# Second attention of a two-block transformer kernel: a convolution moved into the first step, an inverse root merged, three steps shifted

## What is computed

```
h = concat([meta(16), pad, x]); h += concat([mla, diff, swa](rms_norm(h) @ w_in)) @ w_out
h += (silu(hn @ w_gate) * (hn @ w_up)) @ w_down;  x = rms_norm(h, final_norm)[meta:]
h = rmsnorm(x);  q, k, v = split(silu(causal_depthwise_conv(h @ w_qkv)))      # second block
o_dn = gated_deltanet(q, k, v, z, b, a)                                      # 8 heads of 128
o_ns = gates * (compressed, selected, window attention of 16 heads of 64)
x += (sigmoid(g1) * (o_dn @ w_dn) + sigmoid(g2) * (o_ns @ w_ns)) @ w_out
x += square(relu(rmsnorm(x) @ w_up)) @ w_down
```

## Time and profile before

| | us |
|---|---|
| median of 3 runs (lowest to highest) | 957.08 (955.95 to 958.02) |
| the profiled execution, its own time | 955.19 |
| its span, first to last instruction | 953.4 |
| PE busy | 922.3 (97%) |
| DVE busy | 636.9 (67%) |
| ACT busy | 466.9 (49%) |
| POOL busy | 156.2 (16%) |
| mean granted clock of TensorE | 0.991 |

### The profile page before, as it was taken

How to read it: one execution, slowest core, us unless ns; L and a number is a source line. 1 busy time by engine, 2 the same in 40 slices (tenths; PEclk the granted TensorE clock), 3 DMA queues, 4 the chain that set the end, 5 groups by cost and what they waited for, 6 DMA issues and landing times. The chain is left out here.

```text
span 953.4 us, 17694 instructions
## 1 busy us (share of the span) xinstructions
PE 922.3 (97%) x6958; PEld 828.8 (87%) x6958; DVE 636.9 (67%) x1338; ACT 466.9 (49%) x925; POOL 156.2 (16%) x111
## 2 busy tenths in 40 slices
PE   9999899999999999997799999999999999999998
PEld 8897688999999989886688888998888899999996
DVE  4657766666556687798997977545966665455543
ACT  6554655545344562753334674354453464454441
POOL 1100000000000015006565315000000022233221
PEclk9999999999999999999799999999999999999999
DMA  6830334556556445646232101022546546555651
GB/s 242 260 128 1 116 128 122 182 183 223 160 191 216 144 140 180 223 157 216 74 127 87 48 14 67 3 69 90 177 175 202 183 147 221 178 177 177 195 182 44
DMA packets 38578, 139.31 MB, mean 146 GB/s; under 512 B 4325, under 2 KB 4581, under 8 KB 38496
## 3 DMA queue, kind: packets, MB, share of 16 engines
q1 hardware_dynamic: 37152, 134.10, 42.9%
q10 hardware_dynamic: 816, 2.25, 0.7%
q0 software_dynamic: 528, 1.84, 0.7%
HBM read 137.09 MB, written 1.08 MB: 145 GB/s over the span
## 5 line engine op out<-in xcount | busy, mean ns | idle before, releaser
L1835 DVE TENSOR_TENSOR parts<-raw,parts 128x1024 fp32r<-128x1024 f32 (+2 forms) x225 | 286.6, 1310 | 131.7 <-ACT parts L1322 127.0
L1322 ACT ACTIVATE parts<-raw 128x1024 fp32r<-128x1024 f32 (+2 forms) x225 | 228.1, 1050 | 115.8 <-PE psum L532 96.3
L530 PE MATMUL psum<-hT,parts 128*128 128x256 f32 (+1 forms) x928 | 264.6, 285 | 14.4 <-DVE scr L2236 13.2
L531 PE MATMUL psum<-hT,parts 128*128 128x256 f32 (+1 forms) x928 | 263.4, 284 | 0.0
L532 PE MATMUL psum<-hT,parts 128*128 128x256 f32 (+1 forms) x928 | 261.6, 282 | 0.0
L530 PEld LDWEIGHTS psum<-hT,parts 128*128 128x128 f32 x928 | 175.5, 189 | 17.9 <-DVE scr L2236 13.4
L532 PEld LDWEIGHTS psum<-hT,parts 128*128 128x128 f32 x928 | 176.9, 191 | 0.0
L531 PEld LDWEIGHTS psum<-hT,parts 128*128 128x128 f32 x928 | 175.9, 190 | 0.6
L530 PE MATMUL psum<-parts,arena_r 128*128 128x512 f32 x344 | 135.1, 393 | 0.9 <-DVE arena_r L1850 0.7
L532 PE MATMUL psum<-parts,arena_r 128*128 128x512 f32 x344 | 134.0, 389 | 0.0
L531 PE MATMUL psum<-parts,arena_r 128*128 128x512 f32 x344 | 133.9, 389 | 0.0
(11 more groups left out here) (328 smaller groups left out, 1211.4 us busy)
## 6 DMA issues: line engine op xcount, KB each, us to landing
raw<-weights SPq DMA_DIRECT2D x247, 512.0 KB, 4.1
raw<-weights SPq DMA_DIRECT2D x4, 384.0 KB, 4.7
X<-x SPq DMA_DIRECT2D x2, 512.0 KB, 5.1
out<-X SPq DMA_DIRECT2D x2, 512.0 KB, 2.6
arena<-lines POOLq DMA_DIRECT2D x1, 768.0 KB, 9.6
cbuf<-consts ACTq DMA_DIRECT2D x1, 561.0 KB, 6.4
arena<-lines POOLq DMA_DIRECT2D x1, 544.0 KB, 7.8
arena<-params ACTq DMA_DIRECT2D x1, 512.0 KB, 5.5
```

Of the source, the lines that this page charges most:

```text
L530: mm(ps, a, c, start=start, stop=False)
L531: mm(ps, a, d, start=False, stop=False)
L1322: signal(A(split_slot(name)[0], whole_piece, ACT.Copy), "first_parts")
L1835: signal(V_.tensor_tensor(second, whole_piece, first.bitcast(F32), ALU.subtract), "split_vector")
```

## The change

```diff
@@ -356,9 +356,7 @@
 
 
         CONVOLVED = [(w, p, first, n) for w, p in (("v", 1), ("q", 2)) for first in (0, 4) for n in range(2)]
-        EARLY = CONVOLVED[:1]
-        FILLERS = CONVOLVED[1:]
-        FILL = [0, 1, 3, 4, 7, 10, 13]
+        FILL = [0, 0, 1, 3, 4, 7, 10, 13]
         DECAYS = [15, 17, 19, 21]
         n_maps = 0
         for i, g in enumerate(G1 + G2):
@@ -827,13 +825,13 @@
             features("dq1", "dk0", "dk1")
             freed(pe, "p1_dq1")
             freed(pe, "p1_dk1")
-            attention(G1, {0: [values, lambda: freed(pe, "vt_1")],
-                           1: [lambda: features("sq0", "sq1")],
+            attention(G1, {0: [values],
+                           1: [lambda: freed(pe, "vt_1"), lambda: features("sq0", "sq1")],
                            2: [lambda: features("sq2", "sk")],
                            3: [lambda: limited("in1_kr"), lambda: features("kr"), lambda: latent_heads([0, 1])],
                            4: [lambda: latent_heads([2, 3])],
                            5: [lambda: latent_heads([4, 5])],
-                           6: [lambda: limited(None), latent_values, mixed_dif],
+                           6: [latent_values, lambda: limited(None), mixed_dif],
                            7: [lambda: out1_part(0, 0)],
                            8: [lambda: out1_part(0, 1)],
                            9: [mixed_swa],
@@ -1079,8 +1077,6 @@
             two_tokens("vsw", "nv")
             keys_turned()
             conv_half("k", 0, 4, 1)
-            for what in EARLY:
-                conv_half(*what)
             freed(pe, "kcT")
             for k in range(KD):
                 freed(pe, f"nqT_{k}")
@@ -1107,7 +1103,9 @@
                 closed(last, name)
 
             pairs = [(t, q) for t in range(TT) for q in range(2)]
-            extra = {i: [lambda w=what: conv_half(*w)] for i, what in zip(FILL, FILLERS)}
+            extra = {}
+            for i, what in zip(FILL, CONVOLVED):
+                extra.setdefault(i, []).append(lambda w=what: conv_half(*w))
             extra |= {i: [lambda w=what: decay_rows(*w)] for i, what in zip(DECAYS, pairs)}
             extra[DECAYS[0]].insert(0, decay_sums)
             attention(G2, extra, ahead=2)
@@ -1618,8 +1616,9 @@
                 full(act, f"nkT_{b}")
                 release(A(KT[:, 2 * b:2 * b + 2, :], bank_of(f"nkT_{b}"), ACT.Copy, scale=par("k_slc" if b == 0 else "k_win")),
                         f"nkT_{b}")
-            for half in range(4):
+            for half in range(3):
                 silu_conv(0, 4 * (half // 2), half % 2)
+            conv_pieces(0, 4, 1)
             E4 = dn["DT"].rearrange("p (g n) -> p g n", g=4)
 
             def decay_exponents():
@@ -1633,11 +1632,13 @@
                 freed(act, f"gr_{g // 2}_{g % 2}")
                 signal(A(E4[:, g, :], E4[:, g, :], ACT.Exp), "dec_exp")
 
-            extra = {i + 1: [lambda w=what: conv_pieces(*w[1:])] for i, what in zip(FILL, FILLERS)}
+            extra = {}
+            for i, what in zip(FILL, CONVOLVED):
+                extra.setdefault(i + 1, []).append(lambda w=what: conv_pieces(*w[1:]))
             extra |= {i + 1: [lambda g=g: decays(g)] for g, i in enumerate(DECAYS)}
             extra[DECAYS[0] + 1].insert(0, decay_exponents)
             attention(G2, extra)
-
+            silu_conv(0, 4, 1)
 
             full(act, "pv_" + G2[-1]["name"])
             act.dma_start(dn["level"], consts[:, NLATE:NCONST]).then_inc(sem("level_in"), 16)
@@ -1652,7 +1653,7 @@
                         signal(ins, "key_squares")
                     else:
                         release(ins, name)
-            for what in EARLY + FILLERS:
+            for what in CONVOLVED:
                 silu_conv(*what[1:])
             first_parts(INDEX["gn0.0"] + 1)
             z_out(0)
@@ -2094,8 +2095,8 @@
                     if G1[i - 1]["kind"] == "swa":
                         sinks_in(G1[i - 1])
                     finish_one(G1[i - 1])
-                if i in (2, 4):
-                    sublayer_norm((i - 2) // 2)
+                if i in (2, 5):
+                    sublayer_norm(i // 5)
             finish_one(G1[-1])
             mixed_rest(range(YM, KD))
             for nh in range(2):
@@ -2137,7 +2138,7 @@
 
             def tile_scaled(t):
 
-                v0, v1, y = st[:, 30 + t:31 + t], st[:, 28 + t:29 + t], st[:, 6 + t:7 + t]
+                v0, v1, y = st[:, 62 + t:63 + t], st[:, 28 + t:29 + t], st[:, 6 + t:7 + t]
                 a, b = st[:, 8:9], st[:, 9:10]
                 dve.wait_ge(sem("sq3"), 4 * t + 4)
                 link(V_.scalar_tensor_tensor(out=v0, in0=st[:, 2 * t:2 * t + 1], scalar=EPS, in1=st[:, 2 * t + 1:2 * t + 2],
@@ -2275,10 +2276,11 @@
 
             dve.wait_ge(sem("kc_norm"), 1)
             link(V_.tensor_reduce(st[:, 64:80], nsa["Z"][:, 0:1024].rearrange("p (h d) -> p h d", d=ND), AXX, ALU.add))
-            inv_rms(st[:, 80:96], st[:, 64:80], ND, st[:, 128:144], st[:, 160:176])
+            link(V_.tensor_scalar(st[:, 64:80], st[:, 64:80], 1.0 / ND, EPS, ALU.mult, ALU.add))
+            inv_sqrt(st[:, 36:54], st[:, 62:80], st[:, 128:146], st[:, 160:178])
             for t in range(TT):
                 v = nsa["ksw"][:, 512 * t:512 * t + 512].rearrange("p (h d) -> p h d", d=ND)
-                signal(V_.tensor_tensor(v, v, bc(st[:, 80 + 8 * t:88 + 8 * t], [P, 8, ND]), ALU.mult), "nk_norm")
+                signal(V_.tensor_tensor(v, v, bc(st[:, 38 + 8 * t:46 + 8 * t], [P, 8, ND]), ALU.mult), "nk_norm")
             dve.wait_ge(sem("small_ln"), 1)
             link(V_.tensor_scalar(sig[:, :], sig[:, :], 1.0, None, ALU.add))
             link(V_.reciprocal(sig[:, :], sig[:, :]))
@@ -2289,14 +2291,10 @@
             signal(V_.tensor_tensor(gl[:, :, :], soft[:, 0:16].rearrange("p (t h) -> p t h", t=TT),
                                     soft[:, 48:56].unsqueeze(1).to_broadcast([P, TT, NH2]), ALU.mult), "gates")
             convolve("k", 0, 4, 0)
-            second_parts(beyond("cv_k3"))
-            inv_sqrt(st[:, 4:6], st[:, 30:32], st[:, 0:2], st[:, 24:26])
             for t in range(TT):
-                signal(V_.scalar_tensor_tensor(out=X[:, t, :], in0=X[:, t, :], scalar=st[:, 4 + t:5 + t], in1=att1["final"],
+                signal(V_.scalar_tensor_tensor(out=X[:, t, :], in0=X[:, t, :], scalar=st[:, 36 + t:37 + t], in1=att1["final"],
                                                op0=ALU.mult, op1=ALU.mult), "x2")
             convolve("k", 0, 4, 1)
-            for what in EARLY:
-                convolve(*what)
             def finish_two(g):
 
                 c0 = g["first"]
@@ -2352,7 +2350,9 @@
                         step(ins)
 
             pairs = [(t, q) for t in range(TT) for q in range(2)]
-            extra = {i: [lambda w=what: convolve(*w)] for i, what in zip(FILL, FILLERS)}
+            extra = {}
+            for i, what in zip(FILL, CONVOLVED):
+                extra.setdefault(i, []).append(lambda w=what: convolve(*w))
             extra |= {i: [lambda w=what: decay_rows(*w)] for i, what in zip(DECAYS, pairs)}
             extra[DECAYS[0]].insert(0, decay_sums)
             peaks_of(G2[0])
```

## The result

The changed kernel takes 948.12 us (median of 5 runs, 947.15 to 948.90) against 957.68 for five runs of the kernel before beside it. The ratio is 0.9904, 95% interval 0.989 to 0.9917: faster by 9.6 us where 14.0 were forecast. The time lies inside the range. The profiled execution took 947.47 (before: 955.19, so 7.7 less), its span is 945.7.

A forecast was written before the change was run, and what follows sets the result against it. PE, busy 97%, bounds the kernel; only its waits can be won, chiefly 13.2 us for DVE, held by POOL's splitting. Terms: -13.1 + 0.1 - 1.4 + 0.4 = -14.0, from 957.08 to 943.1 us; range 940.5 to 949.0.

The forecast's parts named there:

- Terms 1 to 3: Second attention's start: wait for bank 5 gone, -13.1 us; scaling of X earlier, +0.1; PE's faster clock, -1.4.
- Term 4: cv_v0 into step 0: DVE's chain keeps ahead of PE's fifth scores, negations wait for POOL; +0.4 us, lower bound -1.
- the prediction's own sign for this step: cv_v0 into step 0 is mispriced if PE waits for DVE in 455 to 480 by more than 3 us.
- The first rival: DVE becomes the bound in the first steps, negations held by POOL: gain only 9.4, 947.7 us; chance 0.20.
- Term 5: ACT: one silu and a table load move to the second attention's end, done 0.3 us before PE's turn: 0.
- The rival that a drain of 1.38 us comes on top: Table load at the attention's end on ACT has its drain: +1.0 us, 944.1; chance 0.05.
- Term 6: First attention: shorter waits, about 1.0 us for latent values, are waited for again at L1850: 0, bounds -1.5 and +1.
- The last two rivals: Bank 5's wait stays, 957 us, chance 0.03; POOL's lock catches convolutions in banks 4 and 5, 984, chance 0.03.

The follow-up runs named there:

- first_alone: Kernel before with only the three shifts in the first attention (norm, wait for `vt_1` and `limited(None)` one place later): 957.15 us, ratio 1.0001.
- root_early: Kernel before with the two-column inverse root kept, but moved with the scaling of X ahead of the six split pieces: 949.29 us, ratio 0.9925.
- join_alone: Kernel before with only 18 columns in one inverse root and X scaled ahead of six split pieces; cv_v0 stays ahead of the attention: 947.77 us.
- pause8: Changed kernel with one wait added on POOL, ahead of its ninth split piece until DVE has convolved cv_q0: 951.86 us, ratio 0.9949.

## Why the prediction came out as it did

**Terms 1 to 3 held, within half a microsecond.** PE has no idle time ahead of cv_v1, which runs from 453.85 to 459.65, 5.80 us as forecast. The scaling of X stands at 430.34 with 2.48 us, and PE waits 0.23 for the first split piece (forecast: 0.1). The root of 18 columns takes 2.2 us at 419.44. The three terms sum to -14.4, measured -13.97 at 460 and still at 478 (-14.6 against first_alone's trace). root_early shows that POOL's splitting was the reason.

**Term 4 was mis-sized: +0.4 forecast, +6.2 measured in the pair of traces, 4.4 to 4.7 of it the change's.** Its working was right as far as it went. PE's fifth scores came at 460.61, forecast 460.0. The negations of the first three groups took 1.72, 0.17 and 1.44 us, inside the bounds. But the term ended its count at the fifth scores, with "It holds with 1.5 us to spare", and took POOL's lost gap to matter for those three groups alone. DVE went on with no idle time from 459.85 to 493, held until POOL's twelfth piece ended at 482.28, and two convolutions (cv_v3 and cv_q0, steps 3 and 4) met its delay at 479 to 487. In the kernel before, DVE had 1.44 us idle at 473.82, which I read as proof that it catches up. It did catch up in the changed kernel too, at the same place (0.78 us idle at 459.85). What differs is the stretch behind it: in the next 31 us held instructions took 5.2 us too long before and 9.6 now, since the change removes both of POOL's gaps, 11.18 and 3.18 us. The evidence for slack came from the state that the change ends. Nor did the prediction's own sign for this step, more than 3 us of PE waiting for DVE in 455 to 480, come up: PE waits 0.8 us there, and the rest stands right behind 480.

**The first rival, DVE the bound, is what happened** (chance 0.20, 947.7 us; measured 948.1), but not as it was worked out, and that its number fits is luck. It laid 3.6 of its 4.6 us on the fifth scores, with a whole subtraction for each of three negations; those took 1.72, 0.17 and 1.44 us, PE waited 0.34 us there, as before, and the loss came 18 to 26 us later. The other held forms, which neither term nor rival priced, weigh as much: of the 12.5 us, negations have 5.9, the sums of outputs 3.5 and the products and scalings of small columns 3.1. Removing the negations or the sums restores the gain.

**Term 5 held.** The end of the second attention on ACT, and the first turned keys on PE:

```profile
558.87 1.28 ACT L1574 ACT_TABLE_LOAD   x1
560.16 0.63 ACT L1574 ACTIVATE arena<-arena 128x512 f32<-128x512 f32 x1
```

```profile
561.11 1.91 PE L1122 MATMUL psum<-cbuf,arena 128*128 128x128 f32 x16
```

The silu starts 1.29 us after the load began and ends 0.3 before PE's turn, with no wait. The rival that a drain of 1.38 us comes on top (the Trainium skill, ScalarE: Activation LUTs, "What ACT_TABLE_LOAD costs") is not borne out here.

**Term 6 held as a sum (0), not in its parts.** PE's wait for the latent values did not get 1.0 shorter but 0.4 longer (1.9 for 1.5). first_alone and join_alone show that the whole part changes nothing that can be measured.

The range's lower end, added up from the bounds that it names, is 940.2 and not 940.5; nothing hangs on it.

**The last two rivals** fell: the wait did not stay, and convolutions beside POOL took 2.69 us for six steps everywhere.

## What to carry to other kernels

When a long wait goes, ask what the waiting had stopped: here a stalled PE freed no slots, so POOL paused and DVE recovered, and with the wait gone POOL's pause goes too. Count the follow-up for as many steps as the engine stays without idle time, not to the first bank that is in time. Beside a GpSimd that reads SBUF, look for small DVE instructions with SBUF operands only, first of all those just ahead of a release that PE needs, and fold them into an instruction that reads PSUM: here two such edits were worth nearly as much as the change, but 2.4 us without it.

## What was not expected of the hardware

The peaks instruction with scale -1 and minimum costs what it did with maximum (0.29 us for 128 columns), so the negation is free. A hold is passed on: without the negations the next held form, the product of two columns, took 359 ns in the mean of 24 where it took 286. Thirteen us in which POOL split nothing (pause8) made the kernel 3.7 us slower. And one and the same wait of PE, 1.07 us, left the granted clock at 1.00 in one execution and was followed by 0.81 in another, which cost 1.5 us: two traces that differ by that much need a third.
